# Feed-forward input projection of a hybrid decoder trunk: 18 of 22 column tiles as 2x2 blocks with seven block products

## The reference, cut to what matters

```
def rms_norm(x, g):
    y = xf * lax.rsqrt(jnp.mean(xf * xf, axis=-1, keepdims=True) + RMS_EPS)
    return y * g
def swiglu(h, w_in, w_out):
    gate, up = jnp.split(h @ w_in, 2, axis=-1)
    return (jax.nn.silu(gate) * up) @ w_out
x = x + 0.5 * swiglu(rms_norm(x, ffn_norm[l, 0]), ffn_w_in[l, 0], ffn_w_out[l, 0])
```

## Time and profile before

| | us |
|---|---|
| median of 3 runs (2536.33 to 2538.7) | 2537.53 |
| profiled execution, span from first to last instruction | 2530.7 |
| median less that span | 6.8 |
| PE busy in it | 2462.4 (97%) |
| DVE busy | 863.2 (34%) |
| ACT busy | 943.6 (37%) |
| POOL busy | 1011.8 (40%) |

### The profile page before, as it was taken

One profiled execution on the slowest core, in us unless ns is written; L12 is line 12 of the kernel. 1 busy time (PEld: TensorE's weight loads), 2 busy tenths in 40 slices (PEclk: granted clock), 3 DMA queues, 4 the chain that ended last, 5 costly groups with the idle time before them and its releaser, 6 DMA issues.

```text
span 2530.7 us, 44342 instructions
## 1 busy us (share of the span) xinstructions
PE 2462.4 (97%) x17690; PEld 2012.1 (80%) x17706; DVE 863.2 (34%) x1294; ACT 943.6 (37%) x1510; POOL 1011.8 (40%) x485
## 2 busy tenths in 40 slices
PE   8999999998888999999999999999999998999998
PEld 6888886777776788888888888888888677788887
DVE  5222026456663522201333022220153566422200
ACT  4332224634553433322343233332253664433321
POOL 4444443333334444444444444444453102444442
PEclk9999999999999999999999999999999999999999
DMA  4332223210002332332344443332333241233231
GB/s 155 97 99 92 99 79 104 75 47 4 4 4 67 93 99 92 99 99 92 115 132 144 141 134 94 97 99 92 99 100 100 76 135 43 92 100 96 95 100 58
DMA packets 182819, 230.47 MB, mean 91 GB/s; under 512 B 17464, under 2 KB 121048, under 8 KB 182680
## 3 DMA queue, kind: packets, MB, share of 16 engines
q1 hardware_dynamic: 182680, 228.47, 28.3%
HBM read 213.73 MB, written 14.68 MB: 90 GB/s over the span
## 4 chain that ended last, share of the span: by engine, by line
PE 83%; issue 12%; POOL 2%; DVE 1%; ACT 1%; DMA 0%; SPq 0%; POOLq 0%; ACTq 0%; DVEq 0%
PE bank L352 19%; PE bank L354 19%; PE bank L353 19%; PE bank L359 5%; PE bank L361 5%; PE bank L360 5%; POOL w_lo L327 2%; PE bank L1391 1%; PE bank L1349 1%; PE bank L1005 1%; PE bank L1896 1%; PE bank L1412 1%; PE bank L1284 1%; DVE xg_lo L1876 1%; PE bank L1346 0%
## 5 line engine op out<-in xcount | busy, mean ns | idle before, releaser
L327 POOL TENSOR_TENSOR w_lo<-w_raw,w_hi 128x1024 fp32r<-128x1024 f32 x376 | 907.5, 2418 | 1304.8 <-ACT w_hi L322 1297.1
L322 ACT ACTIVATE w_hi<-w_raw 128x1024 fp32r<-128x1024 f32 x376 | 395.2, 1058 | 1003.8 <-PE bank L354 855.9
L352 PE MATMUL bank<-xg_hi,w_hi 128*128 128x512 f32 x1408 | 549.7, 390 | 6.7 <-POOL w_lo L327 5.2
L354 PE MATMUL bank<-xg_hi,w_lo 128*128 128x512 f32 x1408 | 547.9, 389 | 0.0
L353 PE MATMUL bank<-xg_lo,w_hi 128*128 128x512 f32 x1408 | 547.8, 389 | 0.0
L352 PEld LDWEIGHTS bank<-xg_hi,w_hi 128*128 128x128 f32 x1408 | 264.3, 188 | 64.6 <-issue 5.4
L353 PEld LDWEIGHTS bank<-xg_lo,w_hi 128*128 128x128 f32 x1408 | 264.3, 188 | 55.4 <-issue 0.7
L354 PEld LDWEIGHTS bank<-xg_hi,w_lo 128*128 128x128 f32 x1408 | 264.3, 188 | 55.1
L580 DVE TENSOR_TENSOR gate<-bank,rstd 128x512 f32<-128x512 f32 x88 | 56.7, 686 | 638.9 <-PE bank L354 638.9
L352 PE MATMUL bank<-hid_hi,w_hi 128*128 (+1 forms) x704 | 274.4, 390 | 0.0
L353 PE MATMUL bank<-hid_lo,w_hi 128*128 (+1 forms) x704 | 273.9, 389 | 0.0
(11 more groups left out here) (294 smaller groups left out, 2979.6 us busy)
## 6 DMA issues: line engine op xcount, KB each, us to landing
w_raw<-in_ffn_w_in SPq DMA_DIRECT2D x352, 256.0 KB, 3.0
w_raw<-in_ffn_w_out SPq DMA_DIRECT2D x176, 256.0 KB, 2.7
w_raw<-in_w_kv SPq DMA_DIRECT2D x96, 256.0 KB, 3.1
w_raw<-in_rwkv_w_rkv SPq DMA_DIRECT2D x48, 256.0 KB, 2.9
w_raw<-in_attn_w_q SPq DMA_DIRECT2D x48, 256.0 KB, 3.2
k_dram<-stage SPq DMA_DIRECT2D x6, 1024.0 KB, 4.6
v_dram<-stage SPq DMA_DIRECT2D x6, 1024.0 KB, 5.6
keys<-k_dram SPq DMA_DIRECT2D x24, 256.0 KB, 3.4
```

The source lines that it names most:

```text
L322: act.activation(w_hi[:, s, :], w_raw[:, s, :], ACT.Copy).then_inc(w_hi_ready, 1)
L327: pool.tensor_tensor(w_lo[:, s, :], w_raw[:, s, :], w_hi[:, s, :].bitcast(F32), ALU.subtract).then_inc(w_lo_ready, 1)
L352: pe.matmul(o, hi, x_hi, start=start, stop=False)
L354: return pe.matmul(o, lo, x_hi, start=False, stop=stop)
```

## The change

In each feed-forward layer the first two groups (four column tiles, `PLAIN = 2`) stay as they are. The other 18 tiles are multiplied as 2x2 blocks. The token operand is cut in two halves of 256 tokens and, along k, into even and odd tiles; the weight operand into even and odd k and into gate and up. Seven products of blocks (instead of eight) are formed for each of four k pairs, each in three passes: 84 matmuls of 256 columns per tile in place of 48 of 512. They need:

- tokens divided by the root mean square (`normed_dve`: eight products of 512 columns and four sums of 1024, then high parts on ACT and low parts on DVE and POOL), once a layer;
- sums of weight blocks for each chunk (`weight_sums`: four dependent subtractions of 256 elements on DVE, one of them in place in the raw chunk), with high parts on ACT (`weight_his`, 768 elements more), and low parts on POOL (512 elements more) and DVE (256 elements);
- sums of the seven products, half a bank each (`seven` of DVE: eight operations of 256 columns on PSUM and SBUF), in place of the scaling by `rstd`.

A chunk of these tiles has four k tiles for 128 gate and 128 up columns, so two chunks make a tile, and DMA pieces are 512 B instead of 1 KB. The hidden product is stored unsplit (`hid`), starting at the address of the tokens of the plain groups; its high and low parts are made in the output stage, one tile ahead of use in four slots and two extra ones, and the tiles are taken in the order 6 to 21, 0 to 5. Semaphores for keys and values are merged (three waits into one or two), and the scratch for dynamic DMAs is set to 8192.

The core of the diff:

```diff
+        def weight_sums(dve, ph, q, i=None):
+            for h in range(2):
+                dve.wait_ge(w_landed[s][h], plus((c // SLOTS + 1) * 16, i, 16))
+            dve.wait_ge(w_used, plus(c - SLOTS + 1, i, SLOTS))
+            dve.tensor_tensor(t1, b12, b11, ALU.subtract).then_inc(wt_step, 1)
+            dve.wait_ge(wt_step, plus(2 * at + 1, i, 2 * SLOTS))
+            dve.tensor_tensor(t2, b22, t1, ALU.subtract).then_inc(wt_step, 1)
+            dve.tensor_tensor(b12, b22, b12, ALU.subtract)
+            dve.wait_ge(wt_step, plus(2 * at + 2, i, 2 * SLOTS))
+            dve.tensor_tensor(t4, b21, t2, ALU.subtract).then_inc(wt_ready, 1)
+        def weight_last_lo(dve, ph, q, i=None):
+            dve.wait_ge(w_hi_ready, plus(c + 1, i, SLOTS))
+            dve.tensor_tensor(wt_lo[:, s, 2], wt[:, s, 2], wt_hi[:, s, 2].bitcast(F32), ALU.subtract).then_inc(wt_last_ready, 1)
+        def weight_his(act, ph, q, i=None):
+            act.wait_ge(wt_ready, plus(at + 1, i, SLOTS))
+            act.wait_ge(w_used, plus(c - SLOTS + 1, i, SLOTS))
+            act.activation(wt_hi[:, s], wt[:, s], ACT.Copy)
+            act.activation(w_hi[:, s, :], w_raw[:, s, :], ACT.Copy).then_inc(w_hi_ready, 1)
+        def weight_los(pool, ph, q, i=None):
+            pool.wait_ge(w_hi_ready, plus(c + 1, i, SLOTS))
+            pool.tensor_tensor(wt_lo[:, s, 0:2], wt[:, s, 0:2], wt_hi[:, s, 0:2].bitcast(F32), ALU.subtract)
+            split_lo(pool, c, i, SLOTS)
+        def normed_dve(dve, ph):
+            for k in range(KT):
+                dve.scalar_tensor_tensor(xa[:, k // 2, k % 2], x[:, k], col(ph["gain"], k), rstd[:, :],
+                                         ALU.mult, ALU.mult).then_inc(sums_step, 1)
...
+            dve.tensor_tensor(s1, a21, a22, ALU.add).then_inc(sums_step, 1)
+            dve.tensor_tensor(a21, a11, a21, ALU.subtract).then_inc(sums_step, 1)
+            dve.tensor_tensor(s2, s1, a11, ALU.subtract).then_inc(sums_step, 1)
+            dve.tensor_tensor(s4, a12, s2, ALU.subtract).then_inc(sums_step, 1)
 ffn_act
+            for j in range(SLOTS, 2 * SLOTS - 1):
+                split_hi(act, c0 + j)
+            normed_his(act, ph, slice(0, 4))
+            split_hi(act, c0 + 2 * SLOTS - 1)
+            for t in range(2):
+                silu(t)
+            normed_his(act, ph, slice(4, 7))
+            for q in range(3):
+                weight_his(act, ph, q)
 ffn_dve
+            def step(n, i=None):
+                if 2 * n + 5 < WT_CHUNKS:
+                    weight_sums(dve, ph, 2 * n + 5, i)
+                if 2 * n + 4 < WT_CHUNKS:
+                    weight_last_lo(dve, ph, 2 * n + 4, i)
+                if n < 0:
+                    plain(PLAIN - 1)
+                else:
+                    seven(n, i)
+                if 2 * n + 6 < WT_CHUNKS:
+                    weight_sums(dve, ph, 2 * n + 6, i)
+                if 2 * n + 5 < WT_CHUNKS:
+                    weight_last_lo(dve, ph, 2 * n + 5, i)
...
+            normed_dve(dve, ph)
+            plain(0)
+            weight_sums(dve, ph, 0)
+            normed_lo_dve(dve, ph)
+            weight_last_lo(dve, ph, 0)
+            weight_sums(dve, ph, 1)
+            weight_sums(dve, ph, 2)
+            weight_last_lo(dve, ph, 1)
 ffn_pool
+            for c in range(ph["c0"] + LEAD, seven_start(ph)):
+                split_lo(pool, c)
+            normed_lo_pool(pool, ph)
+            with pool.Fori(0, WT_CHUNKS // SLOTS) as i:
+                for q in range(SLOTS):
+                    weight_los(pool, ph, q, i)
 ffn_pe
+            def seven(n, i=None):
+                        for m, ((hi, lo), (x_hi, x_lo)) in enumerate((
+                                (b11, a11), (b21, a12), (b22, s4), (t4, a22), (t1, s1), (t2, s2), (t3, s3))):
+                            o = bank[b + m // 2][:, m % 2 * HT:(m % 2 + 1) * HT]
+                            pe.matmul(o, hi, x_hi, start=k == 0 and m % 2 == 0, stop=False, skip_group_check=True)
+                            pe.matmul(o, hi, x_lo, start=False, stop=False, skip_group_check=True)
+                            last = pe.matmul(o, lo, x_hi, start=False, stop=k == KP - 1, skip_group_check=True)
```

More of the change, by code:

```diff
@@ L537, in ffn_load @@
-            load_chunk(sp, c1 + FT - 1, row_halves(w_out[(FT - 1) * P:FT * P, :]))
-        def ffn_act(act, ph):
[L540 to L551, removed]
+                    for j in range(2):
+                        load_chunk(sp, cs + 2 * u + j, [
+                            (w_in[:, 4 * j:4 * j + 4, h, bass.ds((i * 2 + (u + 2 * PLAIN)) * P, P)],
+                             lambda slot, h=h: slot.rearrange("p (kt g n) -> p kt g n", kt=4, g=2)[:, :, h, :])
+                            for h in range(2)], i, SLOTS)
@@ new lines, in ffn_act @@
+            for t in range(2):
+                silu(t)
+            normed_his(act, ph, slice(4, 7))
+            for q in range(3):
+                weight_his(act, ph, q)
+            for n in range(-1, 2):
+                step(n)
+            with act.Fori(0, 6) as i:
+                for u in range(2):
+                    step(2 + u, i)
+            for n in range(14, TILES):
+                step(n)
+                if n >= TILES - 2:
+                    hid_high(act, ph, n - TILES + 2)
@@ new lines, in ffn_act @@
+            hid_high(act, ph, 2)
+            hid_high(act, ph, 3)
+            for j in range(SLOTS, AHEAD):
+                split_hi(act, c1 + j)
+                hid_high(act, ph, j)
+            with act.Fori(0, 3) as i:
+                for u in range(SLOTS):
+                    split_hi(act, c1 + AHEAD + u, i, SLOTS)
+                    hid_high(act, ph, AHEAD + u, i)
+            for j in range(AHEAD + 3 * SLOTS, FT + LEAD):
+                if c1 + j < CHUNKS:
+                    split_hi(act, c1 + j)
+                if j < FT:
+                    hid_high(act, ph, j)
@@ L582, in evacuate @@
                 for f in range(2):
[L583 to L587, removed]
+                    dve.tensor_tensor(up[:, f], bank[4 * (g % 2) + 2 + f][:, :], rstd[:, :], ALU.mult).then_inc(up_scaled, 1)
                 for f in range(2):
-                    dve.wait_ge(silu_done, plus(base + t + f + 1, i, 4))
@@ L590, in evacuate @@
[L590 to L596, removed]
@@ L644, in ffn_pe, with rows @@
                 pe.wait_ge(v_odd, 2 * KEYS_GROUPS)
-            if peeled(ph):
+            group(c0 + G_CHUNKS, 1, 1)
+            for n in range(2):
+                seven(n)
+            with pe.Fori(0, TILES // 2 - 1) as i:
                 for u in range(2):
-                    group(c0 + G_CHUNKS * (u + 1), u + 1, 1 - u)
-            with pe.Fori(peeled(ph), PAIRS) as i:
-                for u in range(2):
-                    group(c0 + G_CHUNKS * (u + 1), u + 1, 1 - u, i)
-            c1 = c0 + GROUPS * G_CHUNKS
-            def rows(c, k, order, start=False, stop=False, i=None):
-                s = c % SLOTS
-                pe.wait_ge(w_lo_ready, plus(c + 1, i, SLOTS))
-                tile = bass.ds(plus(k, i, SLOTS), 1)
-                for m in order:
-                    if start:
-                        pe.wait_ge(up_scaled, base + FT - (2 if m >= 4 else 0))
-                        pe.wait_ge(hid_lo_ready, base + FT - 2)
-                    last = products(pe, bank[m][:, :], s, m * P, hid_hi[:, tile, :], hid_lo[:, tile, :],
-                                    start, stop)
+                    seven(2 + u, i)
+            def rows(k, start=False, stop=False, i=None):
+                c = c1 + k
+                pe.wait_ge(w_lo_ready, plus(c + 1, i, SLOTS))
+                pe.wait_ge(hid_lo_ready, plus(base + k + 1, i, SLOTS))
+                hi, low = hid_slot(k)
+                for m in range(KT):
+                    if start and m % 4 == 0:
+                        pe.wait_ge(up_scaled, base + FT - (0 if m >= 4 else 1))
+                    last = products(pe, bank[m][:, :], c % SLOTS, m * P, hi, low, start, stop)
                     if stop and m < KT - 1:
```

284 lines of the change are left out of this document (213 added, 71 removed).

## The result

The changed kernel takes 2617.59 us (median, 2614.64 to 2620.43), against 2537.4 us for the kernel before: ratio 1.0316, 95% interval [1.0298, 1.0333], slower by 80 us. The forecast was 2572 us, +35: the right side, less than half the size.

The account below looks back on a forecast made before the run. PE was taken as the bound before, the port shared by DVE and POOL as what limits the changed tiles. Starts and ends of layers, 3 x 10.1 + 2 + 4 x 0.6 = +35 us on 2537.5, gave 2572 us; range 2515 to 2625.

Parts of the forecast that it names:

- PE's pace: In seven-product tiles, matmuls of 256 columns take 0.120 us each, so a tile takes PE 10.08 us instead of 10.88.
- rival 4: In the tiles, 256 columns don't cover a weight load: +6.0 us a tile, 2982 us in all; chance 0.03.
- The lock: In the tiles, DVE operations with two SBUF operands wait until POOL's instruction is through; port floor 10.1 us a tile.
- the hand schedule: One tile's DVE and POOL instructions laid out in turn, from DVE's second low part: 10.8 us a tile.
- The tile: A seven-product tile takes 10.6 us, bounds 10.1 and 11.4, so each gives back 0.28 us instead of 0.80.
- the prediction's own list of DVE's work: DVE per tile: sums 1.6 each, bank work 3.0, silu and product 0.95, low parts 0.34 each: 7.8 us.
- the sum: The prediction's priced times: POOL 7.3 us a tile, 5.3 us a chunk, 0.69 for DVE's low part of a hidden tile.
- The start: At a layer's start, first seven-product tile at +61.6, fourth chunk at +76.9: +10.1 us three times; third feed-forward layer +2.
- The output stage: At a layer's end, 12 output-projection matmuls go first: +0.6 us, four times; splitting the hidden tiles there is hidden.
- (3): In the tiles, the port goes worse: 11.4 us a tile, +22.9 three times, +15, +2; 2624 us, chance 0.12.

Follow-up runs that it names:

- the experiment with POOL idle: Against the kernel without POOL's low parts of weight sums: POOL splits only two columns in seven-product chunks, PE reads the high part instead; 2532.79 us.
- the run with 468.6 us: Against the changed kernel: POOL's low parts of the weight sums left out, PE multiplies the third sum's low part instead; 2541.93 us.

## Why the prediction was off

**PE's pace: right.** Matmuls of 256 columns start 0.120 us apart (16 steps in 1.92 us from the first to the second of these rows), and where PE sets the pace a tile is 10.08 us, both as worked out; rival 4 is out, the load hides.

```profile
1045.06 0.28 PE L884 MATMUL bank<-xa_lo,w_hi 128*128 128x256 f32 x1
1046.98 0.28 PE L885 MATMUL bank<-xa_hi,w_lo 128*128 128x256 f32 x1
```

**The lock: right in kind and in size.** It was foretold from one row (2.29 for 1.28 us), with L590 far above 0.42 us and PE idle on low parts. Taking out POOL's 512-element instructions gives PE its pace back. In the hand schedule the lock costs DVE 2.25 us at a dependent sum, 1.13 at another and 0.2 at the product, 3.6 in all, and measured it is 3.6.

**The tile: the step that failed.** The hand schedule gave 10.8 us, and the prediction took "10.6, three quarters of the way to the schedule: some small gaps will be used". No gap was used; it is 11.08. And the schedule itself is 0.3 short. Less the lock's 3.6 us it gives DVE 7.2 us a tile, where the prediction's own list of DVE's work came to 7.8; the difference is in the sums of a chunk, 1.6 us in the list and 1.3 in the schedule. The trace has 1.6 for such sums where nothing holds them up (922.27 to 923.82), and 7.4 to 7.5 for the tile (11.08 less 3.6). So two terms were mis-sized, the discount by 0.2 us and DVE's own work by 0.3.

The same 11.08 us can be read as a loop through three engines, off the rows above: POOL's four instructions take 8.15 us (1.54 + 2.40 + 1.73 + 2.58 less overlaps; the sum had 7.3 from undisturbed rows, but POOL waits for DVE too); the released sum and the two behind it, 1.06 us from POOL's end at 1051.72 to ACT's start at 1052.78; ACT's two high parts, 1.87 us to POOL's start at 1054.65. 8.15 + 1.06 + 1.87 = 11.08. The schedule had the two engines and not ACT's leg; POOL idles 2.94 us between two such runs. Over 32 chunks (5.53 us each; the sum had 5.3) the tile's error is +7.2 us a layer.

**The start: the first tile right, what follows it wrong.** The first seven-product tile starts at +60.6 us in the second layer (forecast +61.6) and at +51.7 in the third (forecast +53). But the fourth chunk was to be ready at +76.9 and starts at +80.7, and in the third layer it was forecast at +66 and starts at +71.8. PE, DVE and POOL of the second layer (first matmul at 861.83):

```profile
905.26 0.55 PE L368 MATMUL bank<-xg_hi,w_hi 128*128 128x512 f32 x1 [3.61 <-POOL w_lo L343]
922.45 0.55 PE L883 MATMUL bank<-xa_hi,w_hi 128*128 128x256 f32 x1 [9.83 <-DVE wt_lo L599]
929.83 0.39 PE L883 MATMUL bank<-xa_hi,w_hi 128*128 128x256 f32 x1 [0.54 <-POOL w_lo L343]
936.91 0.36 PE L883 MATMUL bank<-xa_hi,w_hi 128*128 128x256 f32 x1 [1.79 <-DVE up L749]
```
```profile
909.14 2.62 DVE L591 TENSOR_TENSOR w_raw<-w_raw 128x256 f32<-128x256 f32 x1
911.68 2.58 DVE L593 TENSOR_TENSOR wt<-w_raw,wt 128x256 f32<-128x256 f32 x1
914.18 7.83 DVE L647 TENSOR_TENSOR xa_lo<-xa,xa_hi 128x1024 fp32r<-128x1024 f32 x4
926.01 1.52 DVE L588 TENSOR_TENSOR wt<-w_raw 128x256 f32<-128x256 f32 x1
927.57 2.49 DVE L590 TENSOR_TENSOR wt<-w_raw,wt 128x256 f32<-128x256 f32 x1
936.69 3.88 DVE L742 TENSOR_TENSOR hid<-gate,up 128x512 f32<-128x512 f32 x2
```
```profile
906.34 7.64 POOL L653 TENSOR_TENSOR xs_lo<-xs,xs_hi 128x1024 fp32r<-128x1024 f32 x3 [1.13 <-ACT xs_hi L642]
925.72 1.54 POOL L614 TENSOR_TENSOR wt_lo<-wt,wt_hi 128x512 fp32r<-128x512 f32 x1 [4.79 <-ACT w_hi L608]
```

POOL's three token low parts hold up three sums, one each. At 922.27 DVE begins the sums of two chunks at once, and from 925.72 POOL takes both chunks' low parts in one run, in which four more sums wait: they take from 926.01 to 934.03, where the four from 922.27 took 1.6 us. Behind them stand the scaling of the second plain group's banks, for which PE waits 1.79 us at its third chunk, and that group's products, 3.88 us for the two (1.28 in the experiment with POOL idle); so the fourth chunk's sums start only at 940.49. The prediction had given the second chunk 2.1 us of delay and those banks none; the first three chunks take 7.39, 7.08 and 5.60 us. In the second layer the fourth chunk is 3.8 us late by this (5.8 in the third).

The granted clock is no part of it. It falls within the 9.8 us in which PE is idle; it is 0.51 over the stretch from 915.7 to 925.7 us, the 1.2 GHz level, and the first 16 matmuls of 256 columns start 0.213 us apart, which is 1.5 us more than at 0.120. But PE then still waits for POOL's low part, which is made at 929.78, so the lower clock delays nothing. In the first layer 21 matmuls start that far apart and in the third 14, and the first chunk takes 7.40 and 7.38 us there. With POOL idle nothing hides it: it is the 2.65 us that the first tile loses in that experiment.

**The other stages.** The output stage costs 0.4 us (forecast 0.6), and the longer queue of splits there is hidden, though a low part of a hidden tile takes DVE 2.2 us in the mean (L673) and not the 0.69 of the sum. The recurrent section's +4.3 us had no term. The clock's records show the half clock in it for 37.5 us in all, where the kernel before has 30.7; the difference is one stretch of 17.1 us from 799.8 for one of 10.2 from 776.1, which would be some 3 us. The change doesn't bring this by itself: with POOL idle the section has 30.7 us at the half clock and takes 457.2 us, as before, and in the run with 468.6 us it has 58.0. Why the clock stayed down for longer wasn't tested.

Against the forecast's +35: 32 us in three layers, +12 in the third layer, +4.3, and -0.8 in the output stages come to +48, and the spans differ by 47 more. Of the rivals, (3) had the nearest total (2624), with a dearer tile (11.4) and the starts as forecast. Its cause is not what the rows show: outside the bank work lie one POOL instruction of 512 elements and one of 1024, as many as in the schedule. That its total is near is luck, a tile 0.3 us too dear against starts that were too cheap.

## What to carry to other kernels

Two engines that hold each other up must be scheduled as one row, and an engine busy 49% can set the pace: count where the long instruction of one falls among the other's, for only work that doesn't use the port hides it (here the operations on banks). Put the port's work on the engine that does it faster (512 elements: 0.53 us on DVE, 1.5 to 1.7 on POOL), and let the slower engine's instructions run back to back, so that one wait covers them and the bank work the rest; closing a 0.23 us gap on DVE moved them apart and cost 0.41 us a tile. In a loop of three engines, add up the loop's legs; give the schedule every cost that was priced before it, and don't discount it.

## What the runs showed of the hardware

- A matmul of 256 columns costs 0.120 us and one of 512 0.2267 us, the same 0.0133 us on top of the columns at 2.4 GHz. Weight loads of 188 to 193 ns don't show in either. At 1.2 GHz the 256 columns cost 0.213 us, with nothing on top. That costs time only where PE waits for nothing else: 2.65 us in a first tile with POOL idle, none in the changed kernel.
- POOL loses to DVE as well: an instruction of 512 elements is 1.27 us alone; L614 takes 1.54 just behind the start of a DVE operation of 256 elements (1054.65), and 1.73 where DVE's product of 512, held up until then, goes through at the same time (1047.43).
- Each DVE instruction waits by itself: behind a run of POOL instructions, DVE gets one instruction through between two of them (L588, then L590; three sums for three L653), so a row of short operations loses one POOL instruction each. They need not depend on one another: L591 doesn't read what L590 writes, and behind L653 it took 2.62 us all the same.
